# Eight of 22 up-projection steps as seven half-block products on one Trainium2 core

## What is computed

```
def conv_ffn(h, w_up, conv_w, conv_b, w_down):
    S = h.shape[1]
    u = h @ w_up                                  # 512 x 1024 @ 1024 x 5632
    up = jnp.pad(u, ((0, 0), (CONV_W - 1, 0), (0, 0)))
    u = conv_b + sum(conv_w[j] * up[:, j:j + S] for j in range(CONV_W))
    gate, val = jnp.split(u, 2, axis=-1)
    return (jax.nn.silu(gate) * val) @ w_down     # 512 x 2816 @ 2816 x 1024

# in each layer, h = rms_norm(x, g)
x = x + m
x = x + conv_ffn(rms_norm(x, norm_ffn[layer]), ...)
```

## Time and profile before

| | us |
|---|---|
| median of 3 runs (1190.48 to 1192.66) | 1191.71 |
| the profiled execution | 1191.57 |
| its span | 1189.8 |
| PE busy | 1174.8 |
| DVE busy | 862.7 |
| ACT busy | 617.0 |
| POOL busy | 348.5 |

### The profile page before, as it was taken

How to read it: one execution, slowest core, us unless ns; L and a number is a source line. 1 busy time by engine, 2 the same in 40 slices (tenths; PEclk the granted TensorE clock), 3 DMA queues, 4 the chain that set the end, 5 groups by cost and what they waited for, 6 DMA issues and landing times.

```text
span 1189.8 us, 18961 instructions
## 1 busy us (share of the span) xinstructions
PE 1174.8 (99%) x6874; PEld 999.6 (84%) x6874; DVE 862.7 (73%) x1502; ACT 617.0 (52%) x1033; POOL 348.5 (29%) x429
## 2 busy tenths in 40 slices
PE   9999999999999999999999999999999999999998
PEld 7768886778888888888999887988888888888998
DVE  6588968945766566579897898855766666579986
ACT  6554337855434333345565789945534334335563
POOL 0633547830042522211000366730042421211000
PEclk9999999999999999999999999999999999999999
DMA  7555352253398785436554110053387574326553
GB/s 281 182 187 199 142 202 65 73 142 106 106 238 238 199 217 184 175 109 211 186 160 138 62 37 2 1 125 107 106 192 179 156 172 130 106 71 208 176 173 127
DMA packets 51555, 174.54 MB, mean 147 GB/s; under 512 B 4720, under 2 KB 6128, under 8 KB 41504
## 3 DMA queue, kind: packets, MB, share of 16 engines
q1 hardware_dynamic: 36352, 127.51, 31.3%
...
...
## 4 chain that ended last, share of the span: by engine, by line
PE 93%; DVE 3%; ACT 2%; issue 1%; POOL 0%; DVEq 0%; ACTq 0%; POOLq 0%
PE ps L2554 28%; PE ps L2556 27%; PE ps L2555 27%; PE ps L2269 3%; PE ps L2253 3%; PE ps L2069 1%; PE ps L2520 1%; PE ps L2110 1%; PE ps L2237 1%; PE ps L2140 1%; ACT probs L977 1%; DVE w_lo L1705 1%; DVE xT L1725 0%; PE ps L2121 0%; ACT w_hi L1148 0%
## 5 line engine op out<-in xcount | busy, mean ns | idle before, releaser
L2554 PE MATMUL ps<-h_hi,w_hi 128*128 128x512 f32 x704 | 274.4, 390 | 0.0
L2555 PE MATMUL ps<-h_lo,w_hi 128*128 128x512 f32 x704 | 273.9, 389 | 0.0
L2556 PE MATMUL ps<-h_hi,w_lo 128*128 128x512 f32 x704 | 273.9, 389 | 0.0
L1394 DVE TENSOR_TENSOR w_lo<-raw,w_hi 128x2048 fp32r<-128x2048 f32 (+1 forms) x62 | 123.0, 1984 | 118.3 <-ACT w_hi L887 118.3
L1216 ACT ACTIVATE cv<-u_in,vec 128x512 f32<-128x512 f32 x88 | 71.2, 816 | 180.4 <-DVE u_in L1835 178.3
L887 ACT ACTIVATE w_hi<-raw 128x2048 fp32r<-128x2048 f32 (+1 forms) x72 | 121.8, 1692 | 69.1 <-PE ps L2556 69.1
L2554 PEld LDWEIGHTS ps<-h_hi,w_hi 128*128 128x128 f32 x704 | 132.2, 188 | 27.6 <-issue 0.7
L2556 PEld LDWEIGHTS ps<-h_hi,w_lo 128*128 128x128 f32 x704 | 132.2, 188 | 27.6
L2555 PEld LDWEIGHTS ps<-h_lo,w_hi 128*128 128x128 f32 x704 | 132.2, 188 | 27.3
L762 POOL TENSOR_TENSOR v<-act 128x256 f32<-128x256 f32 x16 | 43.3, 2707 | 345.2 <-DVE act L1872 345.2
L2554 PE MATMUL ps<-a_hi,w_hi 128*128 128x256 f32 (+1 forms) x440 | 138.9, 316 | 2.2 <-DVE a_lo L1709 2.2
...
## 6 DMA issues: line engine op xcount, KB each, us to landing
...
w_sums<-in_f_w_down POOLq DMA_DIRECT2D x44, 512.0 KB, 9.0
raw<-w_sums SPq DMA_DIRECT2D x44, 512.0 KB, 4.2
...
raw<-in_f_w_down SPq DMA_DIRECT2D x22, 512.0 KB, 3.9
...
```

Source lines behind the costliest of these rows:

```text
L1394: dve.tensor_tensor(w_lo[:, s, 0:n], raw[:, s, 0:n], w_hi[:, s, 0:n].bitcast(F32), ALU.subtract)\
L2554: pe.matmul(dst, s_hi, m_hi, start=start, stop=False)
L2555: pe.matmul(dst, s_hi, m_lo, start=False, stop=False)
L2556: return pe.matmul(dst, s_lo, m_hi, start=False, stop=stop)
```

## The change

Four steps of each layer (`SEVENS`: steps 5 to 8 in layer one, 2 to 5 in layer two) are made as a 2 x 2 block product with seven half products. Rows are the two channel kinds (gate, value), the inner split is feature tiles 0 to 3 and 4 to 7, columns are the two halves of the tokens (256 each). A product j has its own quarter of weights (a "unit" of 1024 words, `hi4`, `lo4` with four slots), 2 parts x 4 tiles x 3 = 24 matmuls of 256 columns, so a seven step has 168. All steps now take their weights in such units; a plain step has four, a seven step seven.

- *Sums of weights* for the seven steps are made in HBM (`w_two`, `w_more`): eight copies of 1 MB a layer, four accumulations of 1 MB (`two_up`) and eight of 0.5 MB (`three_up`, `four_up`). Layer one's copies stand on GpSimd's queue where the first copies of `w_sums` stood, its accumulations ahead of and in steps 0 and 1. Layer two's copies (`copy_up`) are issued by SyncE in the first input projection and attention, `two_up` by GpSimd in the first down stage, `three_up` and `four_up` in the second attention.
- `copy_weights` moves to steps 1 to 3 of layer one and, for layer two, into the second attention. `sum_weights` is spaced one each two units. `gate_sums` of pairs 3 to 10 waits for the last seven step.
- *Sums of features*: ACT scales the eight tiles (`gained_features`), DVE makes four sums (`sums_of_features`), ACT and DVE their high and low halves (`sum_hi`, `sum_lo`). These are made once a layer, two steps and one step ahead of the first seven step.
- *Results* of a seven step: three PSUM banks (0, 1, 2 and 3, 6, 7 in turn). ACT copies partial sums out between products (`keep`), DVE adds them up (`first_row`, `second_row_sum`, `second_row`), and `second_row`, taps and gating of a seven step are done in the step after it.
- ACT and DVE gate both blocks at once (1024 wide), `rbc_minus` is a negated copy of the inverse norms, and the four loops of the up stage are written out.

```
...
+SEVENS = ((5, 6, 7, 8), (2, 3, 4, 5))
...
+                    load(U_UP[l] + s, f_up[l, 0, s], raw[:, s, :], s)
+                for m, (i, j) in enumerate(UP_UNITS[l]):
+                    r = m % 4
+                    sp.wait_ge(w_lo_done, U_UP[l] + (1 + m // 2 if m < 4 else m - 1))
+                    if i in SEVENS[l]:
+                        z = SEVENS[l].index(i)
+                        if z == 0 and j in (1, 2, 5):
+                            sp.wait_ge(up_sums, sums_made(l, {1: 3, 2: 4, 5: 5}[j]))
+                        src = (f_up[l, i, 0, :, 0:D], w_two[l][z][:, D:2 * D], w_more[l][z][:, 0:D], f_up[l, i, 0, :, D:2 * D],
+                               w_two[l][z][:, 0:D], w_more[l][z][:, D:2 * D], f_up[l, i, 1, :, D:2 * D])[j]
+                    else:
+                        src = f_up[l, i, j // 2, :, (j % 2) * D:(j % 2 + 1) * D]
+                    sp.dma_start(raw4[:, r, :], src).then_inc(f_raw[r], 16)
                 for u in range(G_UNITS):
...
+            def sums_of_first():
+
+                for z in range(len(SEVENS[0])):
+                    two_up(0, z)
+                behind(0, 0, 1)
+                for z in range(len(SEVENS[0])):
+                    three_up(0, z)
+                behind(0, 0, 3)
+                for z in range(len(SEVENS[0])):
+                    four_up(0, z)
...
+                for i in range(7, G_PAIRS):
+                    gate_sums(0, i)
+                for z in range(len(SEVENS[1])):
+                    pool.wait_ge(r_used[1], 4 * z + 3)
+                    two_up(1, z)
+
+            def sums_of_second():
+
+                for k in range(FT):
+                    behind(1, *UP_UNITS[1][2 * k])
+                    if k in (4, 8, 12):
+                        gate_sums(1, k // 4 - 1)
+                    sum_weights(1, k)
+                for i in range(3, G_PAIRS):
+                    gate_sums(1, i)
 
             mask_bias(1)
...
+                def keep(i, j):
+
+                    x, _, v_bank = seven_banks(l, i)
+                    bank, dst = {0: (x, kept[:, 0].rearrange("p (a n) -> p a n", a=2)),
+                                 1: (v_bank, kept[:, 1].rearrange("p (a n) -> p a n", a=2)),
+                                 2: (x, u_in[:, 0:2, 2 + HS:2 + S]), 4: (x, u_in[:, 2:4, 2 + HS:2 + S])}[j]
+                    z = SEVENS[l].index(i)
+                    sc.wait_ge(f_done, DONE_AT[l][i] + j + 1)
+                    if j < 2 and z:
+                        sc.wait_ge(f_in, IN_AT[l][i - 1] + j + 1)
+                    if j >= 2:
+                        sc.wait_ge(f_t0, 2 * FT * l + 4 * (i - 1) + j)
+                    sc.activation(dst, both(ps[:, bank, :]), ACT.Copy).then_inc(f_snap, 1)
+
...
+                def seven_step(i):
+
+                    m, behind = unit_of(l, i), i - 1 in SEVENS[l]
+                    if behind:
+                        tap2(i - 1, 2)
+                        tap2(i - 1, 3)
+                    keep(i, 0)
+                    unit_hi(l, m + 4)
+                    if behind:
+                        silu(i - 1)
+                    keep(i, 1)
+                    unit_hi(l, m + 5)
+                    keep(i, 2)
+                    unit_hi(l, m + 6)
+                    unit_hi(l, m + 7)
+                    keep(i, 4)
+                    unit_hi(l, m + 8)
+                    unit_hi(l, m + 9)
+                    tap2(i, 0)
+                    tap2(i, 1)
+                    unit_hi(l, m + 10)
...
+            def sums_of_features(l, part):
+
+                if part == 0:
+                    dve.wait_ge(t_gained, LANDED + KD * l + 4)
+                    dve.tensor_tensor(t_raw[0], x11, x12, ALU.subtract).then_inc(t_summed, 1)
+                    dve.wait_ge(t_gained, LANDED + KD * (l + 1))
+                    dve.wait_ge(t_summed, LANDED + 4 * l + 1)
+                    dve.tensor_tensor(x12, x22, x12, ALU.subtract).then_inc(t_summed, 1)
+                else:
+                    dve.wait_ge(t_summed, LANDED + 4 * l + 2)
+                    dve.scalar_tensor_tensor(x11, x12, -1.0, x11, ALU.mult, ALU.subtract).then_inc(t_summed, 1)
+                    dve.wait_ge(t_summed, LANDED + 4 * l + 3)
+                    dve.scalar_tensor_tensor(x21, x11, -1.0, x21, ALU.mult, ALU.subtract).then_inc(t_summed, 1)
+
+            def sum_lo(l, j):
+
+                dve.wait_ge(t_hi_ok, LANDED + 4 * l + j + 1)
+                dve.tensor_tensor(quarters(t_lo[j]), t_raw[j], quarters(t_hi[j]).bitcast(F32), ALU.subtract)\
+                    .then_inc(t_lo_ok, 1)
+
+            def unit_lo(l, m):
+
+                if m >= len(UP_UNITS[l]):
+                    return
+                r = m % 4
+                dve.wait_ge(w_hi_done, U_UP[l] + 2 + m + 1)
+                dve.tensor_tensor(lo4[:, r, :], raw4[:, r, :], hi4[:, r, :].bitcast(F32), ALU.subtract)\
...
+                def plain_step(i):
+
+                    m = unit_of(l, i) if i else -4
+                    if i - 1 in SEVENS[l]:
+                        second_row(i - 1)
+                        unit_lo(l, m + 3)
+                        taps(i - 1, (0, 1))
+                        taps(i - 1, (2, 3))
+                        gated(i - 1)
+                    scaled(i, 0)
+                    scaled(i, 1)
...
+                        sums_of_features(l, 0)
+                        sums_of_features(l, 1)
+                    if i == SEVENS[l][0] - 1:
+                        for j in range(4):
+                            sum_lo(l, j)
                     taps(i, (2, 3))
-                    if last:
+                    if i == UP_STEPS - 1:
                         third(l, 1)
                         seven_lo(l, 1, 0)
                         seven_lo(l, 1, 1)
-                    dve.wait_ge(f_t0, 2 * FT * l + 4 * i + 4)
...
+                    gated(i)
+                    if i < UP_STEPS - 1:
+                        unit_lo(l, m + 6)
+                        unit_lo(l, m + 7)
+
+                def seven_step(i):
+
+                    m, behind = unit_of(l, i), i - 1 in SEVENS[l]
+                    if behind:
+                        second_row(i - 1)
+                        unit_lo(l, m + 3)
+                        taps(i - 1, (0, 1))
+                    unit_lo(l, m + 4)
+                    if behind:
+                        taps(i - 1, (2, 3))
+                    unit_lo(l, m + 5)
+                    first_row(i, 0)
+                    if behind:
+                        gated(i - 1)
+                    unit_lo(l, m + 6)
+                    second_row_sum(i)
+                    unit_lo(l, m + 7)
+                    unit_lo(l, m + 8)
+                    first_row(i, 1)
+                    unit_lo(l, m + 9)
...
+                def seven_step(i):
+
+                    banks, z = seven_banks(l, i), SEVENS[l].index(i)
+                    halves = [[h_hi[:, 0:4, 0:HS], h_lo[:, 0:4, 0:HS]], [h_hi[:, 4:8, 0:HS], h_lo[:, 4:8, 0:HS]],
+                              [h_hi[:, 4:8, HS:S], h_lo[:, 4:8, HS:S]]] \
+                        + [[quarters(t_hi[j]), quarters(t_lo[j])] for j in range(4)]
+                    for j, (b, moving) in enumerate(((0, 0), (2, 3), (0, 4), (1, 1), (0, 5), (2, 2), (0, 6))):
+                        m = unit_of(l, i, j)
+                        r = m % 4
+                        pe.wait_ge(w_lo_done, U_UP[l] + 2 + m + 1)
+                        if z == 0 and moving >= 3:
+                            pe.wait_ge(t_lo_ok, LANDED + 4 * l + moving - 2)
+                        if z == 0 and j == 0:
+                            pe.wait_ge(rbc_ok, l + 1)
+                        if z == 1 and j == 0:
+                            pe.wait_ge(f_in, IN_AT[l][i - 1])
+                        if z > 1 and j in (0, 1, 3):
+                            pe.wait_ge(f_in, IN_AT[l][i - 2] + {0: 5, 1: 3, 3: 1}[j])
+                        if j in (2, 4, 5, 6):
+                            pe.wait_ge(f_snap, LANDED + SNAP_AT[l][i] + {2: 1, 4: 3, 5: 2, 6: 4}[j])
+                        for part in range(2):
+                            for k in range(4):
+                                at = k * 2 * P + part * P
+                                ins = product3(pe, ps[:, banks[b], part * HS:(part + 1) * HS], hi4[:, r, at:at + P],
+                                               lo4[:, r, at:at + P], halves[moving][0][:, k],
+                                               halves[moving][1][:, k], j in (0, 1, 3) and part == 0 and k == 0,
+                                               part == 1 and k == 3, True)
+                        ins.then_inc(f_done, 1)
...
```

379 lines of the change are left out of this document (275 added, 104 removed).

## The result

The kernel before took 1192.01 us (1190.48 to 1192.66), the changed one **1201.01 us** (1199.79 to 1202.01): a ratio of 1.0077 with the interval [1.0059, 1.0094], **9.0 us slower** where +5.8 was forecast (1197.4, its own range 1194 to 1201, the whole range 1187 to 1206). The profiled executions span 1189.8 and 1200.2 us.

The account below looks back on a forecast made before the run. The prediction took TensorE (PE), busy 99% of the span, as the bound. Its terms, -13.1 + 10.2 + 0.5 + 3.7 + 4.2 + 0.3 = +5.8 us, gave 1197.4 us; own range 1194 to 1201, whole range 1187 to 1206.

Parts of the forecast that it names:

- first seven step, two layers: PE waits 5.1 us in each layer for product 2's weight quarter, queued on DVE behind the sums' low halves: +10.2 us.
- sums two steps ahead, layer one / two: Feature sums on DVE two steps before the first seven step delay PE: +0.5 us layer one, +3.7 us layer two.
- clock behind the three waits: After each of three PE pauses of 3.7 to 5.1 us, one half-clock stretch losing 1.4 us: +4.2 us in all.
- GpSimd's issues, second attention: Three DMA issues right ahead of a 512-wide unit's normalisation, each costing 0.1 us: +0.3 us.
- the fall at 666 us: The one clock fall in the earlier trace: half clock at 666 to 668 us, some 3 us, after PE idled 1.41 us.
- the walk along VectorE's queue: Adding up DVE's in-order instructions before the wanted weights: ready at T + 10.8 us, wanted at T + 5.75 (T: previous step's end).
- No clock fall: Rival: PE keeps 2.4 GHz through the pauses, +1.6 us, 1193.2 us; chance 0.18.
- short waits: Rival: DVE reaches the wanted quarter 2.5 us or more earlier at three places, clock holds: 1185.7 us; chance 0.14.
- the row taken (0.1198): Measured pace of 256-column products in the down stage, 0.1198 us each, used for seven steps: 20.13 us each, -13.1 us total.
- DMA ... 0: Seven steps need 21.8 us of DMA in 20.1; priced at 0 as long as loads are served first.
- tightest place: ACT's snapshot of bank x in a seven step, ready at 5.2 us, wanted at 5.75; priced 0, bounds 0 and 1.
- DMA full in the seven steps: Rival: each of eight seven steps runs at the DMA queues' 21.8 us, not 20.13: 1206 us; chance 0.16.

Follow-up runs that it names:

- run 5: Changed kernel with feature sums and their low halves moved to other places in VectorE's queue, the wanted weight quarter ahead of the gate: 1183.60 us, ratio 0.9922.
- runs 5 and 6: The second adds to run 5: GpSimd issues no DMA between the 384-wide and 512-wide normalisation of a head pair in the second attention; 1183.14 us, ratio 0.9918.
- run 9: Adds to the second of runs 5 and 6: each of 44 down-weight accumulations moves 16 of 128 partitions (down stage computes other numbers); 1181.98 us, ratio 0.9912.

## Why the prediction was right, and where its sum was off

| term | forecast | measured in the traces |
|---|---|---|
| products, eight seven steps | -13.1 | -13.6 (2 x (87.08 - 80.26)) |
| first seven step, two layers | +10.2 | +9.7 (4.83 each over the pace) |
| sums two steps ahead, layer one / two | +0.5 / +3.7 | +0.2 / +3.5 |
| clock behind the three waits | +4.2 | +6.1 (2.3, 1.7, 2.1) |
| GpSimd's issues, second attention | +0.3 | +1.0 |
| traffic beside the first projection | none | +1.5 |
| GpSimd's additions in steps 9 and 10 | none | +1.0, and 0.3 of the down stage's start |
| the fall at 666 us | stays | -1.3 in this execution |

With small waits for the snapshot (0.4), the first attention (0.2) and the start (1.15, no effect), these lines make +10.1 of the 10.4 us between the profiled spans; 0.3 us are spread over products and marks. The measured median, 1201.01 us, stands at the upper end of the forecast's own range. What the sum left out or had too small adds up to 7.2 us (clock, issues, first projection, additions, first attention, start, snapshots); what it had too large, and the fall that did not come, take 2.8 off. That the number came this near is in part this balance, and the missing fall is luck of this execution.

**Right: the mechanism and three of its sizes.** PE waited where, for whom and, within 0.5 us, as long as the walk along VectorE's queue said, and moving that work, with one quarter of the weights put ahead of the gate, took the kernel from 1201.01 to 1183.60 us (run 5; ratios 1.0077 and 0.9922). *No clock fall* and *short waits* fell with it. **The pace** of a 256-wide product is 0.1194 us; the row taken (0.1198) was a little too dear, half of a wide product (0.1134) too cheap, and the gain of 19 us estimated from the Trainium skill (TensorE: Matmul & The Clock Gate, "Back-to-back issue gap") would have been 5 us too high.

**Off: the stretch at half clock.** The step that failed is "I take one such stretch for each long pause", of 1.4 us after the one at 666 us. The stretches behind the two waits of 4.67 us lasted 5.1 and 4.7 us, not 3, and lost 2.3 and 2.1; the one behind the wait of 3.38 lost 1.7. The price of a product in it was right: 0.213 us each (21 from 417.17 to 421.65), which no row of the kernel before shows.

**Off: GpSimd's part.** "GpSimd's queue ... 0.1 us each" counted what the case in the earlier trace rows left over. The three places lose 0.22 to 0.45 us each. And the prediction counted `gate_sums` nowhere: the change moved these additions in among VectorE's instructions. The error is counting GpSimd's work as free because GpSimd has time.

**Missed: DMA ahead of the seven steps.** "DMA ... 0" was argued for the seven steps themselves, and there it nearly held in the changed kernel, probably because PE's long waits gave the queues time, which no run isolates. In runs 5 and 6, without those waits, 0.2 to 0.9 us per layer come up as waits for ACT's snapshot, the "tightest place" of the walk, and run 9 shows that the traffic makes them. The stretch in which four accumulations of 1 MB meet the loads of the first projection was not looked at. *DMA full in the seven steps* (1206 us) was wrong in size: at a share of 1.02 what is late costs these tenths, not 1.1 us in each of eight steps.

What stays open: why the clock fell behind one pause of 2.4 us and not behind the others, and whether VectorE's lost time in steps 9 and 10 could be placed where nobody waits; only one other place was tried.
